# Order of the first feed-forward panel's products, and two of its mixing steps on GpSimd

## The reference

```python
# first block: SwiGLU, hidden width 2816
h2 = _modulate(_rms_norm(x_new, norm2_g), sh2, sc2)
x_new = x_new + g2 * (silu(h2 @ w_gate) * (h2 @ w_up)) @ w_down
# second block: squared ReLU, hidden width 4096
f = rmsnorm(h, pre_ff_g) @ w_ff1
h = h + rmsnorm(square(relu(f)) @ w_ff2, post_ff_g)
```

## Time and profile before

| what | value |
|---|---|
| time, median of 3 runs | 2500.69 us (2496.49 to 2500.88) |
| the profiled execution | 2507.9 us, its span 2505.7 us |
| TensorE (PE) busy | 2392.7 us, 95% |
| VectorE (DVE) busy | 1567.3 us, 63% |
| ScalarE (ACT) busy | 1036.3 us, 41% |
| GpSimd (POOL) busy | 258.0 us, 10% |
| mean granted TensorE clock | 0.977 |
| SwiGLU stage, first product of panel 0 | 771.64 us |
| squared-ReLU stage, first product of panel 0 | 1862.29 us |

### The profile page before, as it was taken

How to read it: one execution, slowest core, us unless ns; L and a number is a source line. 1 busy time by engine, 2 the same in 40 slices (tenths; PEclk the granted TensorE clock), 3 DMA queues, 4 the chain that set the end, 5 groups by cost and what they waited for, 6 DMA issues and landing times.

```text
span 2505.7 us, 40944 instructions
## 1 busy us (share of the span) xinstructions
PE 2392.7 (95%) x15691; PEld 2050.3 (82%) x15691; DVE 1567.3 (63%) x2612; ACT 1036.3 (41%) x1972; POOL 258.0 (10%) x253
## 2 busy tenths in 40 slices
PE   5799999999898999999999999999979999999998
PEld 2798888788797888888888898899968888788886
DVE  3632327778768777777668923234287777666677
ACT  1422226676523332332444432433255444444444
POOL 0566310000101000000000100012040000000002
PEclk8899999999998999999999999999989999999999
DMA  9233330000331232232666421110313444477553
GB/s 322 70 118 117 118 84 9 2 2 27 110 127 68 81 126 93 97 125 77 228 198 199 162 68 43 35 35 35 135 68 111 167 139 156 147 256 235 151 176 118
DMA packets 191115, 290.32 MB, mean 116 GB/s; under 512 B 11736, under 2 KB 112028, under 8 KB 190620
## 3 DMA queue, kind: packets, MB, share of 16 engines
q1 hardware_dynamic: 190940, 287.94, 34.7%
HBM read 221.56 MB, written 67.34 MB: 115 GB/s over the span
## 4 chain that ended last, share of the span: by engine, by line
PE 66%; DVE 3%; DMA 2%; issue 1%; POOL 1%; ACT 1%; SPq 0%; POOLq 0%; DVEq 0%; ACTq 0%
PE ps L1519 9%; PE ps L1520 9%; PE ps L1521 9%; PE ps L1761 6%; PE ps L1762 6%; PE ps L1763 6%; PE ps L403 4%; PE ps L404 4%; PE ps L405 4%; PE ps L1982 1%; PE ps L1984 1%; PE ps L1983 1%; PE ps L1411 1%; DMA stage<-w_out 0%; PE ps L2554 0%
## 5 line engine op out<-in xcount | busy, mean ns | idle before, releaser
L403 PE MATMUL ps<-w_hi,ht_hi 128*128 128x256 f32 x1488 | 435.3, 293 | 21.2 <-DVE w_lo L388 14.8
L404 PE MATMUL ps<-w_lo,ht_hi 128*128 128x256 f32 x1488 | 426.6, 287 | 0.0
L405 PE MATMUL ps<-w_hi,ht_lo 128*128 128x256 f32 x1488 | 426.3, 287 | 0.0
L403 PEld LDWEIGHTS ps<-w_hi,ht_hi 128*128 128x128 f32 x1488 | 290.9, 196 | 42.8 <-issue 20.1
L404 PEld LDWEIGHTS ps<-w_lo,ht_hi 128*128 128x128 f32 x1488 | 291.4, 196 | 0.5 <-issue 0.5
L405 PEld LDWEIGHTS ps<-w_hi,ht_lo 128*128 128x128 f32 x1488 | 291.1, 196 | 0.0
L1761 PE MATMUL ps<-ff_b_hi,ff_a_hi 128*128 128x512 f32 x448 | 174.5, 390 | 3.3 <-issue 2.1
L1763 PE MATMUL ps<-ff_b_hi,ff_a_lo 128*128 128x512 f32 x448 | 174.3, 389 | 0.0
L1762 PE MATMUL ps<-ff_b_lo,ff_a_hi 128*128 128x512 f32 x448 | 174.3, 389 | 0.0
L1519 PE MATMUL ps<-ht_hi,swiglu_w_hi 128*128 128x512 f32 x352 | 137.3, 390 | 2.4 <-DVE swiglu_gate L1558 2.4
L1722 ACT ACTIVATE ff_a_hi<-ff_a_raw 128x512 fp32r<-128x512 f32 x112 | 70.7, 631 | 165.9 <-PE ps L1763 148.8
(11 more groups left out here) (371 smaller groups left out, 5792.0 us busy)
## 6 DMA issues: line engine op xcount, KB each, us to landing
ff_a_raw<-ff_act_dram SPq DMA_DIRECT2D x112, 256.0 KB, 2.8
stage<-w_in SPq DMA_DIRECT2D x23, 1024.0 KB, 5.3
swiglu_a_raw<-swiglu_act_dram SPq DMA_DIRECT2D x77, 256.0 KB, 2.9
stage<-w_mod SPq DMA_DIRECT2D x16, 1024.0 KB, 5.4
ff_stage<-w_ff SPq DMA_DIRECT2D x16, 1024.0 KB, 5.5
ff_act_dram<-ff_act_sums SPq DMA_DIRECT2D x16, 1024.0 KB, 4.3
ff_act_dram<-ff_acts SPq DMA_DIRECT2D x16, 768.0 KB, 5.8
swiglu_stage<-w_gate SPq DMA_DIRECT2D x11, 1024.0 KB, 6.3
```

Source lines behind the costliest of these rows:

```text
L403: pe.matmul(bank, a, wh[:, k, :], start=(k == 0), stop=False)
L404: pe.matmul(bank, a, wl[:, k, :], start=False, stop=False)
L405: mm = pe.matmul(bank, b, wh[:, k, :], start=False, stop=(k == KT - 1))
```

## The change

The change acts on panel 0 of both stages. Its products run in the order P1, P2, P3, P5, P7, P6, P4 (`FIRST`), and the groups of row pieces are renumbered to match: group 1 is now P5's, 2 is P7's, 3 is P6's; group 0 (P3's) and 4 (P4's) stay. Groups 1 and 2 need only `mix_first`. TensorE no longer turns groups 0 to 2 in one go: each product stands ahead of the last piece of the next group (or of the last pieces). Pieces 12 to 19 take turns in banks 4 to 6 only, so that P6 can use bank 7; P7 goes to bank 0 and waits for `keep`, P4 to bank 4. All `mix_second`s and `mix_third`s are made by GpSimd (`blocks_pool`), after the last `root_row`, one after the other; the first waits for all four `mix_first`s. On VectorE the last two `mix_first`s stand around group 0's `block_lo`s. The third of the early weight blocks is P3's instead of P6's. The joins keep their order.

```diff
+        FIRST = (P1, P2, P3, P5, P7, P6, P4)
...
+            def late_at(e):
+                return 4 + (e % 4 if e < 12 else (e - 12) % 3)
+            def place_of(q, b):
+                return 7 * q + (FIRST.index(b) if q == 0 else b)
+            def w_at(q, b):
+                return {P6: P3, P3: P6}.get(b, b) if q == 0 else b
...
-                    pe.wait_ge(f.mixed, f0.mixed + (8 + j + 1, 2 * j + 1, 2 * j + 2, 12 + j + 1)[g - 1])
+                    pe.wait_ge(f.mixed, f0.mixed + (2 * j + 1, 2 * j + 2, 8 + j + 1, 12 + j + 1)[g - 1])
...
-            def mix_second(dve, j):
+            def mix_second(pool, j):
                 a, d = half(j, 0), half(4 + j, 1)
-                dve.wait_ge(f.turned, f0.turned + 4 + j + 1)
-                dve.wait_ge(f.mixed, f0.mixed + 2 * j + 2)
-                dve.tensor_tensor(d, d, a, ALU.subtract).then_inc(f.mixed, 1)
+                pool.wait_ge(f.turned, f0.turned + 4 + j + 1)
+                pool.wait_ge(f.mixed, f0.mixed + 8 + j)
+                pool.tensor_tensor(d, d, a, ALU.subtract).then_inc(f.mixed, 1)
...
             def bank(q, b):
+                if q == 0:
+                    return ps[:, (0, 1, 7, 3, 0, 2, 4)[b], :]
                 return ps[:, (7 * q + b) % 4, :]
...
-                    pe.wait_ge(f.lo7, f0.lo7 + {P1: 4, P2: 4, P6: 12, P5: 16, P7: 20, P3: 8, P4: 24}[b])
-                if 7 * q + b >= 4:
+                    pe.wait_ge(f.lo7, f0.lo7 + {P1: 4, P2: 4, P3: 8, P5: 12, P7: 16, P6: 20, P4: 24}[b])
+                    if b == P7:
+                        pe.wait_ge(f.kept, f0.kept + 1)
+                elif q == 1 and b < 4:
+                    pe.wait_ge(f.joined, f0.joined + JOINED[(P5, P7, P2, P3)[b]])
+                else:
...
+            for j in range(3):
+                f.turn_block(pe, 1, j)
             pe.wait_ge(dense_evac, evac)
+            f.product(pe, 0, P3)
+            f.turn_block(pe, 1, 3)
+            for j in range(3):
+                f.turn_block(pe, 2, j)
+            f.product(pe, 0, P5)
+            f.turn_block(pe, 2, 3)
+            for j in range(3):
+                f.turn_block(pe, 3, j)
+            f.product(pe, 0, P7)
+            f.turn_block(pe, 3, 3)
+            f.turn_block(pe, 4, 0)
+            f.turn_block(pe, 4, 1)
             f.product(pe, 0, P6)
+            f.turn_block(pe, 4, 2)
+            f.turn_block(pe, 4, 3)
+            f.product(pe, 0, P4)
...
+        def blocks_pool(pool, f):
+            for j in range(4):
+                f.mix_second(pool, j)
+            for j in range(4):
+                f.mix_third(pool, j)
...
-            for b in (P7, P3, P4):
+            for b in (P7, P6, P4):
                 f.weight_hi(act, 0, b)
             f.tick_act(act, 0, P1)
+            for j in range(4):
+                f.block_hi(act, 2, j)
             f.tick_act(act, 0, P2)
-            for g in (2, 3, 4):
+            for g in (3, 4):
...
-            for b in (P1, P2, P6, P5):
+            for b in (P1, P2, P3, P5):
                 f1.weight_hi(act, 0, b)
                 if b == P2:
                     square(4)
```

More of the change, by code:

```diff
@@ L1406, in turn_block @@
                 else:
-                    pe.wait_ge(f.mixed, f0.mixed + (8 + j + 1, 2 * j + 1, 2 * j + 2, 12 + j + 1)[g - 1])
-                pe.wait_ge(f.lo7, f0.lo7 + (3 + j // 2 if g == 0 else e + 1))
-                source = (half(4 + j, 1), half(4 + j, 1), half(j, 0), half(4 + j, 0), half(j, 1))[g]
+                    pe.wait_ge(f.mixed, f0.mixed + (2 * j + 1, 2 * j + 2, 8 + j + 1, 12 + j + 1)[g - 1])
+                held = [x for x in range(e) if late_at(x) == late_at(e)]
+                pe.wait_ge(f.lo7, f0.lo7 + (3 + j // 2 if g == 0 else 4 + held[-1] + 1))
+                source = (half(4 + j, 1), half(j, 0), half(4 + j, 0), half(4 + j, 1), half(j, 1))[g]
                 for k in range(4):
-                    mm = pe.transpose(ps[:, 4 + e % 4, k * P:(k + 1) * P], source[:, k * P:(k + 1) * P], ident[:, :])
+                    mm = pe.transpose(ps[:, late_at(e), k * P:(k + 1) * P], source[:, k * P:(k + 1) * P], ident[:, :])
                 mm.then_inc(f.turned, 1)
@@ L1487, in weight_sum @@
                     if q:
-                        dve.wait_ge(f.w_lo, f0.w_lo + 7 * (q - 1) + 4)
+                        dve.wait_ge(f.w_lo, f0.w_lo + 7 * (q - 1) + (6 if q == 1 else 4))
                     out, x, y, op = w_s1[:, :, :], a21, a22, ALU.add
@@ L1530, in keep @@
             def keep(act, q):
-                act.wait_ge(f.made, f0.made + 7 * q + P1 + 1)
+                act.wait_ge(f.made, f0.made + place_of(q, P1) + 1)
                 if q:
@@ L1541, in join @@
                 made = (P2, P6, P5, P7, P7, P3, P4)[i]
-                dve.wait_ge(f.made, f0.made + 7 * q + made + 1)
+                dve.wait_ge(f.made, f0.made + place_of(q, made) + 1)
                 if i == 0:
@@ L1904, in blocks_dve @@
         def blocks_dve(dve, f):
+            f.mix_first(dve, 2)
             for j in range(4):
-                f.mix_second(dve, j)
                 f.block_lo(dve, 0, j)
+            f.mix_first(dve, 3)
             for j in range(4):
-                f.mix_third(dve, j)
                 f.block_lo(dve, 1, j)
-            for b in (P7, P3, P4):
-                f.weight_lo(dve, 0, b)
-            for g in (2, 3, 4):
+            f.weight_lo(dve, 0, P7)
+            for j in range(4):
+                f.block_lo(dve, 2, j)
+            f.weight_lo(dve, 0, P6)
+            f.weight_lo(dve, 0, P4)
+            for g in (3, 4):
                 for j in range(4):
@@ L2172, in merge_dve @@
             modulate(7)
-            f1.mix_first(dve, 2)
-            f1.mix_first(dve, 3)
             blocks_dve(dve, f1)
@@ L2862, in leave_pool @@
                     f2.root_row(pool, j - 2)
+            blocks_pool(pool, f2)
         def leave_pe(pe):
```

45 lines of the change are left out of this document (18 added, 27 removed).

## The result

The changed kernel took 2510.80 us (median of 7 runs, 2507.70 to 2515.65); the kernel before, measured beside it, 2503.61 us (7 runs, 2496.49 to 2507.93). The ratio is 1.0034, with a 95% interval of 1.0018 to 1.0050: slower by 8.5 us (4.5 to 12.5), where +6.3 us was forecast. (The two medians alone differ by 7.2 us.) The forecast time was 2507.0 us, 3.8 us too low; 2.9 of these are that the kernel before now took 2503.61 us and not 2500.69. The direction, the chain of rounds, the late fifth join and most places came out as forecast. The amount did not: one term, the clock, was taken at little over half its size.

What follows compares the result with a forecast made beforehand. TensorE was taken as busiest by far, with VectorE fuller where the feed-forward stages start. SwiGLU +3.6 us (2.2 + 1.4) and the second stage +2.7 (1.3 + 1.4) gave +6.3, so 2507.0 us from 2500.69; range 2498 to 2512.

Steps and rivals of the forecast that it cites:

- the chain of rounds: Panel 0: product, transposes, copy and block_lo follow singly, 4.9 us a round; SwiGLU's last block_lo +2.2 us, row 5's delay included.
- the late fifth join: SwiGLU stage: thirteen VectorE instructions still follow the last block_lo, so the fifth join and panel 1 come 2.2 us later.
- panel 1 of the squared-ReLU stage: Second stage: the last block_lo, and with it panel 1's start, comes 1.3 us later.
- step 1: SwiGLU stage, ScalarE's queue: P3's early weight copy waits and delays row 5's square and `modulate(5)`, +1.6 us (0 to 2.7).
- step 5: Panel 1's start in the SwiGLU stage: after 5.9 us idle TensorE restarts at half clock, +1.4 us (0 to 2.5).
- that row: Earlier profile's clock row: after similar idle before 786 us, TensorE's clock stayed at 0.51 until 1866 us, 3.7 us of work.
- Relief carries through: Both stages: round waits hide in one another, VectorE gains up to 4.8 us each, 9.6 faster, 2491.1 us; chance 0.12.
- GpSimd late: Rounds of both stages: GpSimd mixing steps over 2.4 us end the rounds, sum +12.7 us, 2513.4 us; chance 0.08.
- No clock loss, step 1 absorbed: Both stages: only the rounds and the joins behind them cost, +1.9 us, 2502.6 us; chance 0.20 with half-way cases.

Runs made afterwards that it cites:

- e2: The changed kernel with panel 1's first two products in spare PSUM banks 5 and 6, waiting for no join; -7.3 us against the kernel before.
- e7: The changed kernel with ScalarE squaring row 5 ahead of P3's and P5's early weight copies in the SwiGLU stage; +9.8 us against the kernel before.
- e3: The changed kernel's order with all second and third mixing steps back on VectorE; +9.8 us against the kernel before.
- e1: The changed kernel with 21 unused matmuls behind panel 0's P4 in both stages; +3.5 us against the kernel before.
- e4: The kernel before, its own order kept, with the second and third mixing steps on GpSimd; -3.8 us against the kernel before.
- e8: e4 with panel 0's three weight splits moved behind group 2's and group 3's last block_lo; -4.0 us against the kernel before.
- e5: e8 with spare PSUM banks for panel 0's P3 and P4, panel 1's first two products and panel 2's first; -9.8 us against the kernel before, 2493.79 us.

## Why the prediction was right, and where it was wrong

The prediction was wrong in the size of one term, the clock's; its mechanism held.

| step | forecast | the profile after |
|---|---|---|
| 1. `modulate(5)` late | +1.6 us | +1.29 (6.35 after `modulate(4)`, 5.06 before) |
| 3. rounds; P4, counted from `modulate(4)` as in before's profile | 810.1 | 804.78 + 5.51 = 810.29 |
| 4. panel 1 of the SwiGLU stage | +2.2 us | +2.34 |
| 5. clock there | +1.4 us | +2.87 |
| panel 1 of the squared-ReLU stage | +1.3 us | +1.10 |
| clock there | +1.4 us | +2.19 |
| sum | +6.3 us | +8.5 |

(5.51 us is by how much `modulate(4)` came sooner: 766.88 against 761.37. The first two rows are contained in the third; the squared-ReLU stage's +1.10 is +1.37 when counted from P2.) That the sum equals the measured 8.5 us is partly luck: it comes from one profile, the interval is 4.5 to 12.5, and from the first product of the SwiGLU stage to the end of the span this profile is only 7.0 us longer. The SwiGLU stage's 5.2 us are still there 650 us later; 1.3 of them are made up before 970 us, in a part that the change leaves alone.

**The placing was right.** P3, P5, P7, P6 came at 788.65, 794.76, 799.66 and 804.74 on before's scale; 789.0, 794.8, 799.7 and 804.6 were forecast. The idle times, 5.87 and 5.18 us, were forecast as 5.9 and 5.3. What was claimed of their cause, the joins behind thirteen VectorE instructions, e2 showed by taking the dependence away. e7 showed step 1. Two small errors cancelled in P4's place: `modulate(5)` came 0.3 us sooner after `modulate(4)` than forecast, and from there to P4 it took 0.5 us longer. VectorE's waits in the rounds came to 7.5 us, not 9.

**The wrong step is step 5, the clock's term**: "a little below that row", 2.8 us at half clock and a cost of 1.4. I can count the loss as the time from panel 1's first matmul to its third product, less the 5.56 and 5.53 us of the kernel before: 8.43 and 7.72 in the changed kernel, so 2.87 and 2.19. The kernel before's third products, for the 5.56 and 5.53:

```profile
822.35 0.39 PE L1519 MATMUL ps<-swiglu_t_hi,swiglu_w_hi 128*128 128x512 f32 x1
```

```profile
1905.99 0.39 PE L1519 MATMUL ps<-ff_t_hi,ff_w_hi 128*128 128x512 f32 x1
```

In e3 the loss is 2.52 and 1.35; in e7 1.31 and 2.20; in e1, where work fills most of the idle time, 0 and 0. Six returns after the same 5.2 to 5.9 us of idle cost 1.3 to 2.9 us, 2.1 on average. The row that I had, 3.7 us of half-clock work, would by itself have given 1.85 a stage and +7.2 in all. I went below it without a reason. The SwiGLU stage's 2.87 us is even outside the 0 to 2.5 that step 5 allowed. The row's neighbour, 9.38 us of work at half clock in the 13 us after 784, had said that more was possible. Of the 2.2 us by which the forecast fell short, this term gives 2.3; the rest nearly cancels.

**The rivals.** *Relief carries through* failed as argued: a round cost 4.9 to 5.6 us, not under 3.7. But e4 shows that there was something in it: without the new order, the relief is worth 3.8 us. I had put the two halves of the change in one sum and never asked what each gave alone; the gain of one was hidden in the loss of the other. *GpSimd late*: its slowest steps took 1.63 us, far from 2.4, and nobody waited. *No clock loss, step 1 absorbed*: the rows at 0.50 exclude the first half, the 1.29 us of step 1 and e7 the second.

**The port.** VectorE's splits of 0.68 us took 1.18 and 1.78 beside GpSimd's steps, while four `block_lo`s, with one input in PSUM, took 2.59 beside them and 2.48 before. In the changed kernel the rounds hid it; in e4 it came through as 1.80 us of TensorE idle. There the single instructions show how, GpSimd's first and VectorE's second and third split after them:

```profile
1868.16 1.62 POOL L1448 TENSOR_TENSOR ff_rows<-ff_rows 128x512 f32<-128x512 f32 x1
1869.86 1.61 POOL L1448 TENSOR_TENSOR ff_rows<-ff_rows 128x512 f32<-128x512 f32 x1
```

```profile
1868.55 1.78 DVE L1480 TENSOR_TENSOR ff_w_lo<-ff_stage,ff_w_hi 128x512 fp32r<-128x512 f32 x1
1870.26 1.76 DVE L1480 TENSOR_TENSOR ff_w_lo<-ff_stage,ff_w_hi 128x512 fp32r<-128x512 f32 x1
```

GpSimd's steps end at 1869.78 and 1871.47, the splits that met them at 1870.33 and 1872.02, each 0.55 us later; and these steps took 1.62 us where the two before took 1.27. The engines took turns, a whole instruction at a time. By the Trainium skill (SBUF — State Buffer, Who interferes with whom) the port that the two share is an exclusive lock, and a VectorE instruction with two inputs in SBUF contends for it with a GpSimd instruction that reads SBUF; these rows agree.

Open: which of the two orders is better once the banks are spare, where the part of e2's and e4's gains lies that their places don't show, why `w_down` comes later once the splits are moved, why the first product of the SwiGLU stage varies by 7 us between executions, and what decides whether a return from idle loses 1.3 us or 2.9.

## What to carry to other kernels

Taking work from a nearly full engine doesn't pay where a chain of single handovers comes in its place; cost the chain, then ask what the last consumer (here the fifth join) waits for, since it decides when the next panel starts. An idle time of TensorE of some 5 us costs itself and then 1.3 to 2.9 us more at half clock, so a spare PSUM bank that bridges it is worth more than the gap shows. And where a profile shows a gain that the total doesn't, as in e8, look for the place further on where it was lost again. Where a change has two halves, price and run each alone.

## What the runs showed of the hardware that was not expected

- The cost of coming back from idle is not fixed: after 5.9 us of idle the SwiGLU stage's panel 1 lost 2.87, 2.52 and 1.31 us in three kernels whose idle there is alike (5.86 to 5.88 us), and after 5.2 us the other stage's lost 2.19, 2.20 and 1.35.
- A short idle time can cost the clock too, and needn't: after 1.92 us in e2 it was 0.57, and 1.7 us were lost; after 2.10 us in e8 it was 0.72, and 1.6 were lost; after 2.22 us at the same place in e5, and after 1.33 us in the kernel before, it stayed at 1.00.
- In the SwiGLU stage ScalarE's table load stands within the run of thirteen instructions: VectorE waits 0.57 us behind it for a weight copy, before and after the change. The chain of waits of the changed kernel shows it (start, duration, what):

```profile
808.31 1.28 ACT L1583
...
810.14 0.62 ACT swiglu_w_hi L1487
...
811.40 0.68 DVE swiglu_stage L1511
812.08 0.61 DVE swiglu_gate L1575
```
